# Two projection chunks stand earlier in a hybrid decoder layer: one ahead of the first turned probabilities, one between the two halves of the samples' weighted values

## What is computed

```python
h = rmsnorm(x, ln1)
proj = h @ w_in                      # 1024 -> 5376 columns = 42 chunks of 128
q, k, v = proj[..., :1536]           # chunks 0 to 11
rc = proj[..., 1536:3328]            # chunks 12 to 25: r, k, v of RWKV, and the inputs of its low-rank parts
gates = proj[..., 3328:]             # chunks 26 to 41: sigmoid gates
o_a = attend(q, k, v)                # prompt: 8 heads; samples: 321 cached keys and values each
xr = rc + (prev - rc) * rwkv_mu
decay, a, g = low-rank products of tanh(xw), xa, sigmoid(xg)
kk = kr * k_k / norm
wkv_T, y = rwkv_scan(...)            # done here in chunks of 32 tokens
mixed = sigmoid(gate_a) * (o_a @ w_branch_a) + sigmoid(gate_b) * (o_b @ w_branch_b)
x = x + mixed @ w_out
x = x + moe(rmsnorm(x, ln2), ...)    # top 4 of 32 experts, every expert's 12 MB of weights are read
```

## Time and profile before

| what | value |
|---|---|
| time, median of 3 runs | 1293.07 us (1291.28 to 1293.76) |
| the profiled execution's own time | 1291.92 us |
| its span | 1290.1 us |
| mean granted clock of TensorE in it | 0.993 of full |
| busy: TensorE matmul / weight load | 1205.4 us (93%) / 594.2 us (46%) |
| busy: VectorE, ScalarE, GpSimd | 341.7, 202.5, 83.9 us |
| DMA | 458.21 MB, mean 355 GB/s |

### The profile page before, as it was taken

One profiled execution on the slowest core, in us unless ns is written; L12 is line 12 of the kernel. 1 busy time (PEld: TensorE's weight loads), 2 busy tenths in 40 slices (PEclk: granted clock), 3 DMA queues, 4 the chain that ended last, 5 costly groups with the idle time before them and its releaser, 6 DMA issues.

```text
span 1290.1 us, 18518 instructions
## 1 busy us (share of the span) xinstructions
PE 1205.4 (93%) x7586; PEld 594.2 (46%) x7586; DVE 341.7 (26%) x657; ACT 202.5 (16%) x413; POOL 83.9 (7%) x57
## 2 busy tenths in 40 slices
PE   7999999989999999999999999999989999999996
PEld 5877689976543333333333333333333333333332
DVE  1068486557321112111112111111111211111112
ACT  3133241420310010101001100100100010010002
POOL 0161002730000000000000000000000000000001
PEclk9999999999999999999999999999999999999998
DMA  9878650133999999999999999999999999999994
GB/s 318 189 248 240 213 191 11 37 113 124 404 384 428 428 429 427 429 429 427 429 428 430 427 429 429 428 428 428 430 427 429 429 430 427 429 429 427 429 428 166
DMA packets 52206, 458.21 MB, mean 355 GB/s; under 512 B 7716, under 2 KB 10428, under 8 KB 27588
## 3 DMA queue, kind: packets, MB, share of 16 engines
q1 hardware_dynamic: 50084, 453.81, 85.6%
q0 software_dynamic: 1296, 3.53, 1.3%
q10 hardware_dynamic: 784, 0.28, 0.1%
HBM read 453.74 MB, written 3.82 MB: 355 GB/s over the span
## 4 chain that ended last, share of the span: by engine, by line
PE 63%; DMA 27%; DVE 3%; ACT 3%; issue 2%; SPq 1%; POOL 0%; DVEq 0%; ACTq 0%; POOLq 0%
PE ps L1801 21%; DMA work<-in_w_gate_up 13%; DMA ring<-in_w_gate_up 13%; PE ps L1829 12%; PE ps L1341 11%; PE ps L1752 4%; PE ps L1784 2%; PE ps L1666 2%; PE ps L1761 2%; PE ps L1515 1%; PE ps L1320 1%; ACT work L743 1%; PE ps L1655 1%; SPq L367 1%; DVE ring L868 1%
## 5 line engine op out<-in xcount | busy, mean ns | idle before, releaser
L1801 PE MATMUL ps<-ring,work 128*64 128x512 f32 x1536 | 341.8, 595 | 20.3 <-DMA ring<-in_w_gate_up 19.7
L1801 PEld LDWEIGHTS ps<-ring,work 128*64 128x64 f32 x1536 | 107.6, 137 | 251.8 <-issue 217.2
L1829 PE MATMUL ps<-ring,work 128*64 128x512 f32 x768 | 170.1, 595 | 18.4 <-ACT work L771 18.4
L1341 PE MATMUL ps<-work,ring 128*128 128x264 f32 x672 | 158.3, 395 | 2.2 <-ACT work L549 2.2
L1254 DVE TENSOR_SCALAR work<-ps 128x512 f32<-128x512 f32 x32 | 22.1, 691 | 464.9 <-PE ps L1801 464.9
L1341 PEld LDWEIGHTS ps<-work,ring 128*128 128x128 f32 x672 | 129.1, 194 | 28.7 <-issue 6.7
L1801 PE MATMUL ps<-work 128*64 128x512 f32 x512 | 114.3, 596 | 6.2 <-DMA work<-in_w_gate_up 6.2
L1829 PEld LDWEIGHTS ps<-ring,work 128*64 128x64 f32 x768 | 53.4, 137 | 119.7 <-issue 104.0
L1273 DVE SCALAR_TENSOR_TENSOR work<-work 128x512 f32<-128x512 f32 x32 | 24.1, 752 | 309.8 <-ACT work L774 309.8
L766 ACT ACTIVATE work<-work 128x512 f32<-128x512 f32 x32 | 20.1, 629 | 502.9 <-DVE work L1254 502.9
L1752 PEld LDWEIGHTS ps<-work 128*128 128x128 f32 x544 | 66.7, 196 | 28.8 <-DVE work L1258 15.2
(11 more groups left out here) (255 smaller groups left out, 897.9 us busy)
## 6 DMA issues: line engine op xcount, KB each, us to landing
ring<-in_w_gate_up SPq DMA_DIRECT2D x96, 2048.0 KB, 31.1
ring<-in_w_down SPq DMA_DIRECT2D x48, 2048.0 KB, 35.2
work<-in_w_gate_up SPq DMA_DIRECT2D x32, 2048.0 KB, 30.9
work<-in_w_down SPq DMA_DIRECT2D x16, 2048.0 KB, 34.5
ring<-in_w_in SPq DMA_DIRECT2D x6, 3072.0 KB, 15.0
ring<-in_w_out SPq DMA_DIRECT2D x1, 4096.0 KB, 13.0
ring<-in_w_in SPq DMA_DIRECT2D x2, 1536.0 KB, 8.2
ring<-in_cache_k SPq DMA_DIRECT2D x16, 192.0 KB, 8.4
```

The costliest lines, as they stand in the source:

```text
L1341: last_ = mm(psum(job, T), WIN[gi % 2][:, k, j * 128:(j + 1) * 128], hT[:, k, :], start=k == 0, stop=k == KD - 1)
L1801: last = mm(PS[bnk][g * 64:g * 64 + 64, :], lhs, UNIT[n % 8][:, w0 + base + g * 512:w0 + base + (g + 1) * 512], start=False, stop=k == KD - 1)
L1829: last = mm(PS[BY][g * 64:g * 64 + 64, :], lhs, UNIT[n % 8][:, w0:w0 + 512], start=k == 0, stop=k == KD - 1)
```

## The change

Nothing is added to or taken from the computation. All 42 chunks are still computed in the order of their numbers; what changes is between which other steps they stand, on TensorE and on ACT, and with that the bank of the jobs between.

- `project(14, 15)` ahead of `turn_probs(0)` becomes `project(14, 16)`. Every single chunk between two heads then has a number higher by one.
- Between `decode(0)` and `decode(1)` stood chunks 25 to 27; now 26 to 29.
- Between the low-rank products and the sums of squares 31 and 32 stand in place of 29 and 30; behind the sums of squares, ahead of sx, stand eight chunks (33 to 40) in place of nine (31 to 39); between sx and the bonus sums stands none in place of chunk 40.

The core of the diff (ACT's program and the list of jobs follow TensorE's in the same way):

```diff
--- before.py
+++ after.py
@@ psum_jobs
-    jobs += pr(14, 15) + ["pt0", "s2"] + pr(16, 16) + ["pt1", "s3"] + pr(17, 17) + ["ov0", "pt2", "s4"]
+    jobs += pr(14, 16) + ["pt0", "s2"] + pr(17, 17) + ["pt1", "s3"] + pr(18, 18) + ["ov0", "pt2", "s4"]
...
@@ block.scalar
-            project(24, 28)
+            project(25, 30)
             act.wait_ge(S_("xr_ready"), 1)
...
-            project(29, 29)
+            project(31, 31)
             act.wait_ge(S_("st_out"), 16 * 6)
-            project(30, 31)
+            project(32, 33)
...
@@ block.tensor
-            project(14, 15)
+            project(14, 16)
             turn_probs(0)
             score(2)
-            project(16, 16)
+            project(17, 17)
             turn_probs(1)
...
-            project(24, 24)
+            project(25, 25)
             decode(0)
-            project(25, 25)
-            project(26, 27)
+            project(26, 29)
             decode(1)
-            project(28, 28)
+            project(30, 30)
             after(pe, "pv0", "pv1")
...
-            project(29, 30)
+            project(31, 32)
             pe.wait_ge(S_("kk_sq"), 1)
...
-            project(31, 39)
+            project(33, 40)
             pe.wait_ge(S_("products"), 1)
             for x in range(2):
                 transposes(f"sx{x}", [svT[:, 4 * x:4 * x + 4].rearrange("p b x c -> p (b x c)")], 128, 96)
-            project(40, 40)
             pe.wait_ge(S_("rk"), 1)
```

More of the change, by code:

```diff
@@ L97, in psum_jobs @@
     jobs += [f"kn{m}" for m in range(NM)] + pr(9, 12) + [f"vn{m}" for m in range(NM)] + pr(13, 13) + ["s0", "s1"]
-    jobs += pr(14, 15) + ["pt0", "s2"] + pr(16, 16) + ["pt1", "s3"] + pr(17, 17) + ["ov0", "pt2", "s4"]
[L99 to L103, removed]
+    jobs += pr(14, 16) + ["pt0", "s2"] + pr(17, 17) + ["pt1", "s3"] + pr(18, 18) + ["ov0", "pt2", "s4"]
+    jobs += pr(19, 19) + ["pt3", "s5"] + pr(20, 20) + ["ov1", "pt4", "s6"] + pr(21, 21) + ["pt5", "s7"]
+    jobs += pr(22, 22) + ["ov2", "pt6", "sst"] + pr(23, 23) + ["pt7"] + pr(24, 24) + ["ov3", "spt"]
+    jobs += pr(25, 25) + ["pv0"] + pr(26, 29) + ["pv1"] + pr(30, 30) + ["sv", "sh"]
+    jobs += [f"{k}{c}" for k in ("lw", "la", "lg") for c in range(4)] + pr(31, 32) + [f"nk{c}" for c in range(4)]
+    jobs += pr(33, 40) + ["sx0", "sx1"] + [f"bo{c}" for c in range(4)] + pr(41, 41)
     jobs += [f"{k}{m}" for m in range(2) for k in ("tV", "tK", "tC", "tB")]
@@ L592, in _ @@
             exponents(1)
-            project(14, 15)
+            project(14, 16)
             turned(0)
             exponents(2)
-            project(16, 16)
+            project(17, 17)
             turned(1)
             exponents(3)
-            project(17, 17)
+            project(18, 18)
             turned(2)
             exponents(4)
-            project(18, 18)
+            project(19, 19)
             turned(3)
             exponents(5)
-            project(19, 19)
+            project(20, 20)
             turned(4)
             exponents(6)
-            project(20, 20)
+            project(21, 21)
             turned(5)
             exponents(7)
-            project(21, 21)
+            project(22, 22)
             turned(6)
-            project(22, 22)
+            project(23, 23)
             turned(7)
@@ L616, in _ @@
             A_.ready(nc.scalar.activation(s64[:64], s64[:64], ACT.Exp, bias=nms[:64], accum_out=lss[:64]), "s_probs", 1)
-            project(23, 23)
+            project(24, 24)
             act.wait_ge(S_("pts_zero"), 1)
@@ L639, in _ @@
                 evacuate(f"lg{c}", gT_[:, c, :], psum(f"lg{c}", T))
[L640 removed]
+            project(31, 31)
             act.wait_ge(S_("st_out"), 16 * 6)
[L642 removed]
+            project(32, 33)
             act.wait_ge(S_("kk_max"), 1)
             A_.ready(nc.scalar.activation(bT, bT, ACT.Sqrt), "kk_norm", 1)
[L645 removed]
+            project(34, 35)
             act.wait_ge(S_("scan_done"), 1)
@@ L657, in _ @@
             A_.ready(nc.scalar.activation(svT[:, :, 0, :].rearrange("p b c -> p c b"), sgs, ACT.Exp, scale=-DECAY), "decays", 5)
-            project(34, 39)
+            project(36, 40)
             for x in range(2):
@@ L661, in _ @@
             act.dma_start(sv_d.rearrange("(i b) x (c p) -> (b x c) i p", i=2, p=128), svn[:96]).then_inc(S_("st_sv"), 16)
-            project(40, 41)
+            project(41, 41)
             for m in range(2):
```

## The result

The changed kernel took 1287.68 us in the median (1283.31 to 1291.16, 12 runs), the kernel before 1295.68 beside it (1291.23 to 1298.40, 12 runs): ratio 0.9937 [0.9922, 0.9953]. Two later series beside other runs of before gave 0.9954 [0.9937, 0.9972] and 0.9947 [0.9928, 0.9967]. The 31 runs of the changed kernel in all its series have a mean of 1287.35, and 65 runs of before in three later series have 1293.61: 6.3 us, with a standard error of 0.55. (With the twelve of before beside the first series, whose clocks are not on record, before has 1293.82 over 77 runs, and the difference is 6.5.) So it is faster, by somewhat more than the 5.1 of the sum.

The account below looks back on a forecast made before the run. TensorE was taken to bound the kernel (63% of the chain, transfers 27%), its idle stretches lying on the path. Gains 6.46, less 0.47 and 0.90, make 5.09; off the median 1293.07 that gives 1288.0, range 1284.5 to 1291.0.

Parts of the forecast that it names:

- the 5.1 of the sum: Predicted total gain: 5.99 us at the 32 transposes, less 0.90 for VectorE's imat steps, 5.09.
- First place: Ahead of the first turned probabilities: a third chunk fills TensorE's 2.60 us wait for VectorE; gain 3.89.
- the new stall at the fourth head: TensorE, arriving earlier at the fourth head's turned probabilities, waits 0.47 us for VectorE, leaving it 0.33 ahead.
- The clock term isn't there: Rival: the 1.61 us of clock behind the first gap is not gained; 3.5 gain, 1289.6; 20 in 100.
- Second place: Ahead of the second half of the weighted values: four chunks cover the 2.41 us wait; gain 6.46 with the first place.
- Weights: Weight loads needed a slot earlier; tightest is group 6 for chunk 36, with 3.0 us of cover, costed at nothing.
- the slower rival: Chunk 36 waits for its weights, group 6 landing late; at 192 it costs 8.8 us, 1296.8; 4 in 100.
- Third place: Around sx: without chunk 40 the bonus sums wait some 0.5 us for `rk`; the transposes start 5.99 earlier.
- The bound that I had set for being wrong: The prediction is wrong if the 32 transposes don't start 5.5 to 6.5 us earlier.
- Fourth place: VectorE's imat steps would start inside GpSimd's second step on the samples and be held up; cost 0.90 us.
- The clock stays high in both places: Rival: filling the second gap also removes the lower clock in the low-rank products; 2.5 us more, 1285.5; 12 in 100.
- No gain at the end: Rival: the expert stream's start doesn't move, or GpSimd's samples' chain comes last; gain 0 to 2, about 1292.5; 10 in 100.

Follow-up runs that it names:

- rep_after: The changed kernel run once more, unaltered, for a second profile: 1286.28 us (12 runs) beside 1293.48 for the kernel before.
- redo_chunk: Kernel before, with chunk 16 computed an extra time ahead of the first turned probabilities, no chunk moved: one execution, 1297.18 us, read for its trace alone.
- second_only: Kernel before with only the second wait filled: four chunks between the two halves, eight ahead of sx: 1287.49 us (6 runs), ratio 0.9951.
- imat_late: Changed kernel with VectorE's two imat steps and the samples' first sum moved behind the four masking steps: 1285.53 us (7 runs), ratio 0.9940.
- redo_second: Kernel before, with chunk 27 computed an extra time ahead of the second half of the weighted values: 1297.37 us (12 runs), ratio 1.0015.
- imat_late_again: The changed kernel with the later imat steps once more, beside the changed kernel on one chip: 1286.71 us against 1286.55, 7 runs each.
- first_only: Kernel before with only the first wait filled: three chunks ahead of the first turned probabilities, one fewer ahead of sx: 1289.49 us (12 runs), ratio 0.9967.
- before_again: The kernel before once more, unaltered, for a second profile: one execution, 1293.28 us.
- changed_again: The changed kernel once more, unaltered, for a third profile, on one chip with the later imat order: 1286.55 us (7 runs).
- keep_chunk40: Changed kernel with chunk 40 put back between sx and the bonus sums, seven chunks ahead of sx: 1288.83 us (12 runs), ratio 0.9955.
- imat_late_before: Kernel before with VectorE's imat steps moved behind the masking steps, as a control: 1293.42 us (10 runs), ratio 1.0001.

## Why the prediction was right, and where it was not

**The forecast held.** 1288.0 was given, 1287.68 measured, inside the range. But this agreement is better than the steps deserve: the runs beside it put before at 1293.5 to 1295.7 where the sum started from 1293.07, and some terms were off in opposite directions. That it comes within 0.3 us is in part luck.

**First place.** The start of the first turned probabilities (+0.81 from chunk 14, as put), the full clock and the second head (put at 88.92, with the 0.43 of the later start 89.35; 89.45 measured) held, and so did the mechanism of the new stall at the fourth head. Its size was 0.60, 0.50 in rep_after, instead of 0.47; in the three profiles of the changed kernel TensorE was between 0.12 behind and 0.25 ahead of before there, put at 0.33 ahead. But the price list attached to it was wrong. I booked "the 2.7 or so of the idle stretch and 1.61 of clock, less 0.47". redo_chunk shows that the 1.61 and the idle stretch are not additive: VectorE's fourth head sets TensorE's place, with or without the fall. By the prediction's own rows, a kernel before without the fall would come to that head 1.61 earlier and be held until 100.22, so the fall was worth 0.33 there at most. What the move brings is the pitch of the chunk, and the rival "The clock term isn't there" was overpriced at 1.6.

**Second place.** The wait is gone as put. In the changed kernel the second half started 0.88 to 1.25 later than before instead of 0.66. All but 0.14 of the rest is the fourth head's, passed on: by itself the place gave its 2.57 (second_only).

**Weights.** Chunk 36 never waited; the slower rival did not occur.

**Third place.** The stall for `rk` was 0.30 in all three profiles of the changed kernel (0.30 and 0.31 in the two of imat_late), put at 0.47. The transposes came 5.33 and 5.70 nearer where the low-rank products had the same clock as before, 5.57 in rep_after less its 3.33; put at 5.99. The bound that I had set for being wrong, 5.5 to 6.5, was missed by 0.17 in the first of these.

**Fourth place: the step that failed in size.** The collision of imat with GpSimd was foreseen, and imat_late, with its control, shows it as the cause. It costs 1.8 to 2.2, not 0.90. The way that I priced it was right: in all three profiles of the changed kernel it costs what is left of GpSimd's step when imat starts, less some 0.15 (2.18 for 2.32 left, 1.77 for 1.93, 2.01 for 2.16). What was wrong is how much is left. Of the two ends, both counted with the 0.43 of the later start, GpSimd's came 2.08 later than I put it (218.29 against 216.21) and imat's start 0.66 later (215.97 against 215.31), so that 0.90 became 2.32. GpSimd started 11.5 behind sx (201.98 to 213.50), where I carried over the 10.0 of before; the other 0.57 is sx itself, which started later. From sx to GpSimd it is 11.1 to 11.5 in all five profiles of kernels without chunk 40 there, and 9.8 to 10.1 in seven of the eight others (11.2 in redo_second). Why the samples' vectors come back later there stays open; in four of these five, and in redo_second, one of SP's sixteen issues of them took 1.0 to 1.6 instead of 0.3. What I did not look for at all is the clock right behind: it was low there in all three profiles of the changed kernel, for another 1.3 in the first (5.15 instead of 3.85). Whether the new idle stretch ahead of it (1.94, 1.54, 1.78) brings that is not settled: with some 1.9 of idle time at the same place, imat_late had low clock and imat_late_again had not, and first_only and before_again had it without any such stretch.

**The rivals.** "The clock stays high in both places" did occur, in rep_after. It was underpriced: the twelve low-rank products take 5.02 at full clock, so it is worth 3.33 and not 2.5. But the filled second gap alone does not bring it. With that gap filled the clock still fell in the low-rank products in the traces of the changed kernel, changed_again, imat_late_again and redo_second, and did not in rep_after, second_only, keep_chunk40 and imat_late: 4 of 8. With the gap there (before, before_again, imat_late_before, redo_chunk; 1.48 of it in first_only) it fell in 3 of 5, in redo_chunk already at 147 to 155, ahead of those products. Thirteen traces can't rule out that the gap makes the fall somewhat more likely. The first gap is another matter: low clock behind it in all five traces that have it, and in none of the eight where it is filled. The rule of the Trainium skill ("TensorE: Matmul & The Clock Gate", What's actually happening), that sustained activity releases the throttle, fits the first place and does not by itself tell the second.

**The gain at the end.** From SP's load at 344.69 to the end it is 945.41 before. The six other traces without low clock at 346 to 362 have the same within 0.2 (the changed kernel's first within 0.13), so what reaches SP reaches the end, and "No gain at the end" is out. But SP's first expert load, put at 5.1 earlier, came 0.99, 5.47 and 2.49 earlier in the three profiles of the changed kernel: in none did the whole lead of the transposes reach SP, since imat and the clock took from it on the way.

**How 6.3 comes about.** Compared at the same mean clock, by a line through each kernel's runs, the changed kernel is 4.4 us faster at 0.992 (1293.6 to 1289.2) and 4.6 at 0.995 (1291.0 to 1286.4). The other 1.8 go with a higher mean clock, 0.9940 against 0.9920. The 4.5 are what the places give (5.3 to 5.7 at the transposes) less imat's 1.8 to 2.2, with about one us that the traces don't attribute. Why the mean clock rises stays open: neither the filled first gap alone (first_only 0.9924) nor busy matmuls in the second alone (redo_second 0.9918) show it, while second_only has 0.9952, of six runs.

## What to carry to other kernels

When a filled wait speeds up one engine, follow the next engine's own ready times to the place where they meet again: only what is left there counts, and time won from the clock ahead of that place may be worth nothing. When two engines move by different amounts, look for their two-operand SBUF steps sliding over each other; there the cheap mend is to reorder the step that has slack. And before reading a gain of half a per cent from one trace, see how far executions of the same kernel differ, and compare them at equal clock.

## What the runs showed of the hardware

- The time of an execution of this kernel follows its mean granted clock: 0.87 us per 0.001 for before, 0.93 for the changed kernel. Runs of one kernel had means of 0.986 to 0.997.
- The clock falls at the same few places, but not in each execution: between 346 and 368, early in the expert stage, in 6 of 13 traces. There it costs 3.7 to 4.1 us between SP's load (at 344.69 in the kernel before) and the end. At 84 to 88 it costs nothing in redo_chunk's comparison, since VectorE is the later one there; where it lasted until 92 (redo_second), the fourth head came 2.4 later, 0.8 of it from a longer wait ahead (3.40 instead of 2.60).
- VectorE's pair of steps with two SBUF operands took 3.60, 3.19 and 3.43 where it started beside a GpSimd step, in the three traces of the changed kernel, and 1.42 in the ten others. It ended 1.26 to 1.28 behind GpSimd's end each time: next to nothing of it was done before.
- The one-operand steps that set TensorE's place in the attention stand beside GpSimd too. L907 took 3.53 at 79.50, where it took 0.35 at 99.81; it ended at 83.03, and this GpSimd block of the kernel before ran until 82.89:

```profile
68.92 13.97 POOL L814 TENSOR_TENSOR ring<-ring,work 128x1536 f32<-128x1536 f32 x4 [7.01 <-DMA ring<-work]
```

The same holds of the fourth head, whose new stall the change brought. Its first step, 0.29 elsewhere, ends 0.08 behind GpSimd's:

```profile
96.26 3.43 POOL L814 TENSOR_TENSOR ring<-ring,work 128x1536 f32<-128x1536 f32 x1 [3.51 <-DMA ring<-work]
96.62 3.15 DVE L906 TENSOR_SCALAR work<-work 128x128 f32<-128x128 f32 x1
```

So the wait of 2.60 that the change fills, and what is left of its gain at the fourth head, may themselves be such collisions. No run moved GpSimd's steps there, so this is not shown.
